# The order of two VectorE steps in a two-layer trunk kernel: a weight unit's low part first, the head norm second

## The reference

```
def _memory_attention(q, mem_n, w_kv, q_g, k_g):
    q = _rmsnorm(q.reshape(b, s, MEM_HEADS, MEM_HEAD_DIM), q_g)
    k, v = jnp.split(mem_n @ w_kv, 2, axis=-1)
    k = _rmsnorm(k.reshape(b, m, MEM_HEADS, MEM_HEAD_DIM), k_g)
    ...
def _sb_mix(h, mem_n, w_in, q_g, k_g, w_out, mem_w_kv, mq_g, mk_g):
    q, k, v, q_mem = jnp.split(h @ w_in, [SB_WIDTH, 2 * SB_WIDTH, 3 * SB_WIDTH], axis=-1)
    q = _rmsnorm(q.reshape(shp), q_g)
    k = _rmsnorm(k.reshape(shp), k_g)
    o = _stick_breaking(q, k, v.reshape(shp)).reshape(b, s, SB_WIDTH)
```

## Time and profile before

| what | value |
|---|---|
| three runs, median (lowest to highest) | 815.62 us (815.34 to 815.93) |
| the profiled execution's own time | 815.59 us |
| its span, first to last instruction | 813.5 us |
| PE busy | 804.1 us (99%) |
| DVE busy | 541.8 us (67%) |
| ACT busy | 437.5 us (54%) |
| POOL busy | 62.9 us (8%) |

### The profile page before, as it was taken

The page is one execution under the profiler, slowest core; times in us unless marked ns, Lnnn a source line. Parts: engine busy times, 40 slices in busy tenths (PEclk is TensorE's granted clock), DMA queues, the critical chain, the costliest instruction groups (busy, mean ns, idle before and its releaser), DMA issues.

```text
span 813.5 us, 9762 instructions
## 1 busy us (share of the span) xinstructions
PE 804.1 (99%) x3858; PEld 672.1 (83%) x3858; DVE 541.8 (67%) x746; ACT 437.5 (54%) x520; POOL 62.9 (8%) x80
## 2 busy tenths in 40 slices
PE   9989999999999999999999999999999999999998
PEld 8977888888888888888888888888888888888886
DVE  6678989997758555455347878578767755555442
ACT  5657775466537444434326576667653744445330
POOL 4000013530000000000000000113220000000000
PEclk9999999999999999999999999999999999999999
DMA  7844466443446656555555545443445556565561
GB/s 242 286 155 157 131 219 213 149 169 105 159 155 205 198 167 204 174 189 191 177 202 171 191 155 158 153 155 105 154 156 155 178 184 200 168 202 171 191 207 52
DMA packets 85292, 141.38 MB, mean 174 GB/s; under 512 B 3406, under 2 KB 50672, under 8 KB 85248
## 3 DMA queue, kind: packets, MB, share of 16 engines
q1 hardware_dynamic: 84256, 139.60, 52.3%
q10 hardware_dynamic: 608, 1.06, 0.3%
q0 software_dynamic: 384, 0.11, 0.1%
HBM read 139.68 MB, written 1.07 MB: 173 GB/s over the span
## 4 chain that ended last, share of the span: by engine, by line
PE 80%; DVE 12%; ACT 3%; issue 2%; DMA 1%; SPq 0%; DVEq 0%; ACTq 0%
PE acc L1253 24%; PE acc L1255 24%; PE acc L1254 24%; PE bank L1250 4%; DVE lo L940 4%; DVE zs L1053 2%; DMA raw<-in_ssd_w_in 1%; ACT hi L627 1%; DVE seg L1073 1%; DVE seg L1081 1%; PE bank L1447 1%; PE bank L1425 1%; DVE hg L1073 1%; ACT sq L627 1%; ACT zs L627 1%
## 5 line engine op out<-in xcount | busy, mean ns | idle before, releaser
L940 DVE TENSOR_TENSOR lo<-raw,hi 128x2048 fp32r<-128x2048 f32 (+2 forms) x132 | 296.5, 2252 | 130.8 <-ACT hi L627 130.6
L627 ACT ACTIVATE hi<-raw 128x2048 fp32r<-128x2048 f32 (+2 forms) x132 | 245.6, 1862 | 72.1 <-DMA raw<-in_ffn_w_down 47.3
L1253 PE MATMUL acc<-lo,aT_hi 128*128 128x512 f32 (+1 forms) x672 | 264.2, 393 | 1.3 <-DVE lo L940 0.9
L1255 PE MATMUL acc<-hi,aT_lo 128*128 128x512 f32 (+1 forms) x672 | 258.9, 385 | 0.0
L1254 PE MATMUL acc<-hi,aT_hi 128*128 128x512 f32 (+1 forms) x672 | 258.4, 385 | 0.0
L1253 PEld LDWEIGHTS acc<-lo,aT_hi 128*128 128x128 f32 x672 | 126.3, 188 | 25.6 <-issue 1.1
L1255 PEld LDWEIGHTS acc<-hi,aT_lo 128*128 128x128 f32 x672 | 126.1, 188 | 25.7
L1254 PEld LDWEIGHTS acc<-hi,aT_hi 128*128 128x128 f32 x672 | 126.4, 188 | 23.8
L1253 PE MATMUL acc<-lo,uT_hi 128*128 128x512 f32 x176 | 68.7, 391 | 0.0
L1255 PE MATMUL acc<-hi,uT_lo 128*128 128x512 f32 x176 | 68.5, 389 | 0.0
L1254 PE MATMUL acc<-hi,uT_hi 128*128 128x512 f32 x176 | 68.5, 389 | 0.0
(11 more groups left out here) (200 smaller groups left out, 869.2 us busy)
## 6 DMA issues: line engine op xcount, KB each, us to landing
raw<-in_ffn_w_gate_up SPq DMA_DIRECT2D x88, 512.0 KB, 4.8
raw<-in_ffn_w_down SPq DMA_DIRECT2D x22, 1024.0 KB, 4.9
raw<-in_sb_w_in SPq DMA_DIRECT2D x20, 1024.0 KB, 5.0
raw<-in_ssd_w_in SPq DMA_DIRECT2D x14, 1024.0 KB, 5.1
raw<-in_mem_w_kv SPq DMA_DIRECT2D x8, 1024.0 KB, 5.0
raw<-in_ssd_w_out SPq DMA_DIRECT2D x8, 1024.0 KB, 4.9
raw<-in_sb_w_out SPq DMA_DIRECT2D x8, 1024.0 KB, 4.9
seg<-cs_rows SPq DMA_DIRECT2D x6, 384.0 KB, 4.7
```

What stands on the lines that cost most here:

```text
L627: return nc.scalar.activation(out_, in_, func, **k)
L940: v.tensor_tensor(lo[w % RING][:, c], raw[w % RING][:, c], hi[w % RING][:, c].bitcast(F), ALU.subtract).then_inc(lo_ready, 1)
L1253: mm(ps, stat_hi, mov_lo, start=first, stop=False)
L1255: return mm(ps, stat_lo, mov_hi, start=False, stop=last)
```

## The change

One line of constants changes. The step `hn` leaves the list of steps that DVE does ahead of its splits and joins the list that comes right behind them. ACT walks through the same two lists, but `hn` is nothing to it.

```
-EARLY, MIDDLE = ("seg", "pn", "zd", "sps", "hn"), ("segm",)
+EARLY, MIDDLE = ("seg", "pn", "zd", "sps"), ("segm", "hn")
```

## The result

The changed kernel takes **824.17 us** (median of five executions, 822.60 to 825.03), the kernel before 815.62 us on the same chip (median of five as well). The ratio is 1.0103, with a 95% interval of 1.0089 to 1.0117: slower by 8.55 us. The forecast was 821.7 with a range of 819.0 to 824.8. The profiled execution took 824.35 us, 0.2 above the median, over a span of 822.3 us.

What follows compares the result with a forecast made beforehand. PE, busy 804.1 of 813.5 us, was taken as the bound, so only its waits count. New waits of 0.6 + 1.0 + 2.2 + 1.0 + 0.9 + 0.4 = 6.1 us on 815.59 gave 821.7 us, range 819.0 to 824.8.

Steps and rivals of the forecast that it cites:

- km0: Head norm of km0: DVE waits 0.6 us for unit 18's high part, so PE starts at 118.0 instead of 117.4: 0.6.
- qm1: Head norm of qm1: unit 73's high part ends at 448.97, so PE starts at 456.45 against 455.42: 1.0 us.
- k1: Head norm of k1: ACT's high part of unit 77 comes late too, PE starts at 483.1 against 480.9: 2.2 us.
- q1: Step q1: DVE idles 0.9 us for the high part, making subtraction L1170 and PE's step O late: 0.9.
- k2: Head norm of k2: score maximum, exponentials and unit 79's high part come later, PE at 497.6 against 496.6: 1.0 us.
- The step that counted ACT's own work: At k1: ACT's block, squares, heads and scores come after PE's, so ACT is 1.0 us late as well.
- only the 2.2 us: Rival, chance 0.09: DVE never waits for a high part, norms end only 2.2 us later, k1 costs 1.5: 817.1 us.
- qm0: Head norm of qm0: transposes end 1.1 us late, but waits at unit 12 and the convolution take that: 0.0.
- The step that failed is the paragraph on the clock: Rival, chance 0.20: PE's clock falls to half within the longer pause at qm0, +2.0 us, giving 823.7.
- Theory A: Formed after the measurement: stalls make about 6 us, falls of the clock behind the two longest pauses the rest.
- Theory B: Formed after the measurement: stalls alone make 8.5 us, each also delaying ACT and DVE; the clock's falls cost nothing.
- What "wrong" would have been: Signs: k1 pause under 2 us, stalls not reaching the trace's end, or PEclk below 1.00 behind 50 us.

Runs made afterwards that it cites:

- all of layer 1 late: Kernel before with only the head norms qm1, k0, k1, k2, q0, q1 and q2 behind the low part; 821.58 us, ratio 1.0076.
- the filled one: Changed kernel plus matmuls of ones, 15 in PE's pause at qm0 and 8 at k1, overwritten by the transposes; 822.24 us, ratio 1.0082.
- qm0 alone: Kernel before with only the head norm of qm0 moved behind the low part; 816.07 us, ratio 1.0010.
- k1 alone: Kernel before with only the head norm of k1 moved behind the low part; 819.64 us, ratio 1.0042.
- the kernel filled at qm0 alone: Changed kernel plus 32 matmuls of ones in PE's pause at qm0, none at k1; 824.13 us.
- the run with `cs` early: Kernel before with DVE's small decay operations L1041 to L1044 ahead of the head norm of qm0; 814.23 us, ratio 0.9977.
- the last run: Kernel before with L1041 to L1044 ahead of qm0's head norm, and that norm one unit up, ahead of the convolution; 813.44 us, ratio 0.9976.

## Why the prediction was right, and where it was short

**The mechanism held.** DVE waits for ACT's high part with the norm queued behind it; DVE's wait at L940 grew from 130.6 to 139.3 us in sum. The forecast of waits, about 9 us at four to six blocks and 1.5 in front of one L1447, came as 8.0 at five blocks and 1.5.

**Term by term**, by the table above: km0 0.56 (0.6), qm1 1.03 (1.0), k0 and q0 no wait (0, 0), k1 2.37 (2.2), q1 0.97 (0.9), q2 0.39 (0.4). k2 added 0.81 (1.0), a little less since PE came later for another reason, the clock; its wait was 0.65, and without a fall 0.76 in the kernel with all of layer 1 late and 0.82 in the filled one. Together 6.1, as forecast. The step that counted ACT's own work (squares, heads, scores) on top of PE's lateness was the one that mattered: the rival *only the 2.2 us* without it gave 817.1, and the kernels with all of layer 1 late, or with the fill, have medians of 821.6 and 822.2.

**qm0** was forecast as 0.0. The pause was right (3.93, forecast 3.9). Of the 0.84 us that PE is late ahead of the scan, 0.48 is there before any head norm, in the landing of the first inputs, which the change does not touch; 0.36 is left for qm0, with a fall. The run with qm0 alone gives 0.4 us by the median, with one fall in most executions. In the filled kernel, without a fall, PE is 0.28 late ahead of the scan (98.63), of which 0.16 is there at 44 us: 0.1 is left, so the stall by itself was forecast rightly.

**The step that failed is the paragraph on the clock.** The forecast put the fall at qm0 as a rival with 0.20 and 823.7, and the likeliest case left it out. It came in every execution of the kernel with qm0 alone late. Its price was read too high (+2.0; measured 0.4 with one fall, and 1.3 for pause and fall together in the trace with a stretch of twice the length), and its chance too low. The price took a third of unit 8's length as lost, 2.4 us, for want of a row; a fall of 3.4 us lost at most 1.7, and most of it at qm0 was taken back. What was not considered at all is a fall at k1: the pause there was forecast at its right length, about 2.2 us, and no fall was priced behind it. The fall there cost 1.5 to 1.7 us. In the profiled execution stalls of 6.1, plus 1.7 at k1, plus 0.4 at qm0, plus 0.5 from the start give 8.7 of its 8.8. Theory A is shown by PE's time from k1's transposes to k2's, 16.0 us with a fall and 14.5 to 14.6 without one, filled or not; the filled pauses (822.24 at a clock of 1.000 against 824.17) and the two groups of executions of k1 alone agree. Theory B falls.

**What "wrong" would have been** was named as PEclk below 1.00 behind 50 us. It was below, at 51.6. So the time fell into the range, but the forecast case as described is not what happened: it was the forecast's stalls together with more of the rival's mechanism. That the range held the result was partly luck: its upper end was there for a fall at qm0, and the fall that cost most came at k1.

The prediction said of the Trainium skill's page "TensorE: Matmul & The Clock Gate", section "What's actually happening", that no run had yet shown the return at busy time. The windows at 51.6 to 55.0 and 485.1 to 488.5 do: PE was busy in 3.40 of 3.40 us at 0.50, and 1.00 followed. By that section activity releases the clock; the trace agrees.

## What to carry to other kernels

An engine that runs its list in order should not have, ahead of a long chain that another engine needs soon, an operation that waits for a third engine and that nobody needs for two units: the price is its duration plus its wait, at every place without slack. When PE gets a new pause, price it twice, once as the pause and once as a possible fall of the clock behind it, and look at the mean granted clock of each execution, since a fall comes in some executions and not in others. When PE's waits don't add up to the loss, compare its busy time for the same instructions.

## What the runs showed of the hardware

- A pause of PE of 2.1 to 2.2 us went with a fall in three of five executions of k1 alone, in one of five of all of layer 1, in one of four of the kernel filled at qm0 alone and in four of eleven with the norm of qm0 moved up; where the fall lay is seen in the profiled executions only. One of 1.67 us with 0.95 soon after was followed by none in the profiled kernel before. The one of 2.7 us in the run with `cs` early had a fall in six of eleven; with the ones of 3.9 and 4.0 us every execution of the changed kernel and of qm0 alone had one at least (mean clock 0.994 to 0.998). What decides in one execution stays open.
- Each fall lasted 3.4 us in these traces, or twice that, and could begin in the pause or up to 1.3 us behind it (50.60 to 51.9 us in the last run). A single one cost between 0.4 us (qm0, later waits took most of it back) and 1.6 us (k1, between the two rows of the traces), less than the 3.4 us it lasted.
- The same kernel's executions differ before they reach any edit: at 44 us the profiled ones stood between 0.2 us earlier and 1.3 us later than the trace of before.
- A 128x128 f32 matmul stands as two records of 0.114 us each in the trace (64 for 32 issued).
